# Scatter of results ahead of gather of tokens: the order of GpSimd's work in the expert loop of a mixture-of-experts layer

## The reference

```python
scores = jax.nn.sigmoid((t @ w_router).astype(jnp.float32))
_, idx = lax.top_k(scores + router_bias.astype(jnp.float32), TOP_K)
...
xb = t[row_tok].reshape(n_blocks, EXPERT_BLOCK, d)

def expert_block(args):
    xblk, e = args
    g, u = jnp.split(xblk @ w_expert_gu[e], 2, axis=-1)
    return (jax.nn.silu(g) * u) @ w_expert_down[e]

yb = lax.map(expert_block, (xb, block_e)).reshape(n_rows, d)
routed = jax.ops.segment_sum(yb * row_w[:, None].astype(yb.dtype), row_tok, num_segments=n_tok)
```

## Time and profile before

| | |
|---|---|
| median of 3 runs | 1791.23 us |
| the profiled execution's own time | 1791.92 us |
| its span | 1790.1 us |
| PE busy | 1711.8 us, 96% |
| DVE, ACT, POOL busy | 64%, 45%, 30% |
| chain that ended last | PE 71%, DMA 14% (of it the scatter 11%), DVE 5% |
| granted clock of PE | 0.991 of full |
| scatters, gathers | 102, 107 |

### The profile page before, as it was taken

One profiled execution on the slowest core, in us unless ns is written; L12 is line 12 of the kernel. 1 busy time (PEld: TensorE's weight loads), 2 busy tenths in 40 slices (PEclk: granted clock), 3 DMA queues, 4 the chain that ended last, 5 costly groups with the idle time before them and its releaser, 6 DMA issues.

```text
span 1790.1 us, 32548 instructions
## 1 busy us (share of the span) xinstructions
PE 1711.8 (96%) x7475; PEld 1239.2 (69%) x7476; DVE 1145.5 (64%) x1692; ACT 799.3 (45%) x1098; POOL 538.3 (30%) x578
## 2 busy tenths in 40 slices
PE   7999999998889999899999999999999999999997
PEld 1545454446754477688887787888888887888874
DVE  4773775403877869657538788654768578275647
ACT  0211112122231032457538787654767577265634
POOL 2000000004832320134334344334444344333442
PEclk9999999999999999999999999999999999999999
DMA  9752000011344241768959899867789789587775
GB/s 381 274 218 96 1 0 0 1 37 42 114 141 177 106 165 54 298 199 290 291 101 357 285 352 343 307 161 222 225 315 332 193 301 367 124 291 206 219 212 201
DMA packets 95503, 357.79 MB, mean 200 GB/s; under 512 B 19389, under 2 KB 19550, under 8 KB 86757
## 3 DMA queue, kind: packets, MB, share of 16 engines
q1 hardware_dynamic: 65298, 288.49, 42.3%
q0 software_dynamic: 30160, 68.76, 17.2%
q10 hardware_dynamic: 4, 0.02, 0.0%
HBM read 330.96 MB, written 70.62 MB: 224 GB/s over the span
## 4 chain that ended last, share of the span: by engine, by line
PE 71%; DMA 14%; DVE 5%; issue 4%; ACT 2%; DVEq 1%; SPq 1%; POOL 1%; ACTq 1%; POOLq 0%
DMA sum_rows<-arena,idxs 11%; PE psum L1356 7%; PE psum L1358 7%; PE psum L1357 7%; PE psum L1082 7%; PE psum L1187 5%; PE psum L1091 4%; PE psum L1343 4%; PE psum L1380 3%; PE psum L1379 3%; PE psum L1378 3%; PE psum L1029 3%; PE psum L1122 3%; DMA raw_weights<-in_w_gu 1%; ACT split_weights L698 1%
## 5 line engine op out<-in xcount | busy, mean ns | idle before, releaser
L1972 DVE TENSOR_TENSOR split_weights<-raw_weights,split_weights (+1 forms) x366 | 428.9, 1221 | 46.8 <-ACT split_weights L698 35.8
L698 ACT ACTIVATE split_weights<-raw_weights (+1 forms) x366 | 364.3, 1060 | 36.5 <-issue 24.3
L1356 PE MATMUL psum<-split_weights,split_rows 128*128 (+1 forms) x832 | 335.7, 403 | 2.3 <-DVE split_rows L1961 2.3
L1358 PE MATMUL psum<-split_weights,split_rows 128*128 (+1 forms) x832 | 325.7, 391 | 0.0
L1357 PE MATMUL psum<-split_weights,split_rows 128*128 (+1 forms) x832 | 324.9, 390 | 0.0
L698 ACT ACTIVATE arena<-psum 128x1024 f32<-128x1024 f32 (+6 forms) x187 | 154.5, 831 | 370.0 <-PE psum L1082 107.1
L654 POOL DMA_INDIRECT sum_rows<-arena,idxs x102 | 177.6, 1741 | 228.6 <-DMA sum_rows<-arena,idxs 186.4
L698 ACT ACTIVATE split_rows<-psum 128x256 fp32r<-128x256 f32 (+1 forms) x209 | 148.2, 710 | 138.4 <-PE psum L1364 124.1
L640 POOL COPY idxg<-idxT 128x1 uint32 (+1 forms) x107 | 72.8, 681 | 365.1 <-DVE split_rows L1961 292.9
L1358 PEld LDWEIGHTS psum<-split_weights,split_rows 128*128 128x128 f32 x832 | 156.8, 188 | 34.6
L1356 PEld LDWEIGHTS psum<-split_weights,split_rows 128*128 128x128 f32 x832 | 157.6, 189 | 31.5 <-DVE split_rows L1961 2.5
(11 more groups left out here) (312 smaller groups left out, 2317.8 us busy)
## 6 DMA issues: line engine op xcount, KB each, us to landing
raw_weights<-in_w_gu SPq DMA_DIRECT2D x62, 2048.0 KB
raw_weights<-in_w_dn SPq DMA_DIRECT2D x62, 1024.0 KB
arena<-in_w_ada SPq DMA_DIRECT2D x12, 2048.0 KB, 8.8
arena<-in_toks SPq DMA_DIRECT2D x18, 512.0 KB, 9.2
arena<-job_rows SPq DMA_DIRECT2D x16, 512.0 KB, 3.8
arena<-in_w_vog SPq DMA_DIRECT2D x1, 4160.0 KB, 14.2
arena<-in_w_qk SPq DMA_DIRECT2D x1, 4096.0 KB, 17.4
arena<-in_w_out SPq DMA_DIRECT2D x2, 2048.0 KB, 9.0
```

Source lines behind the costliest of these rows:

```text
L698: return act.activation(o, i, ACT.Copy)
L1356: mm(bank(3 + p), xk, part(par, 0, 512 * k), start=(k == 0), stop=False)
L1358: ins = mm(bank(3 + p), xl, part(par, 0, 512 * k), start=False, stop=(k == 7))
L1972: tt(cols(wsplit, (1 - par) * (2 * WE) + (WE + 1024 * c), 1024), cols(raw, (1 - par) * WE + 1024 * c, 1024), high, ALU.subtract).then_inc( ...
```

## The change

In the body of the loop, POOL first scatters the result of block b, and then gathers the rows of block b+5; before it was the other way round. The wait for `m_xb` moves with the gather. The counts that the two index copies wait for (6 and 7, before 7 and 6) follow from the order.

```diff
@@ -667,9 +667,9 @@
             with pool.Fori(0, rest) as i:
                 for p in range(2):
 
+                    add_rows(2 * i + p, p, 4 * i + (2 * p + 6), 16 * i + (16 + 16 * p))
                     pool.wait_ge(S("m_xb"), 2 * i + (p + 4))
-                    gather(bass.ds(2 * i + (p + 5), 1), 1 - p, 4 * i + (2 * p + 6))
-                    add_rows(2 * i + p, p, 4 * i + (2 * p + 7), 16 * i + (16 + 16 * p))
+                    gather(bass.ds(2 * i + (p + 5), 1), 1 - p, 4 * i + (2 * p + 7))
```

## The result

The changed kernel takes 1795.9 us (median of 13 runs, 1790.05 to 1802.49), the kernel before 1790.46 us (13 runs, 1787.77 to 1792.38): ratio 1.0029, 95% interval 1.002 to 1.0039. A second series gave 1.0042 (1.0028 to 1.0056). The prediction was 1787.4 us and faster; the result is slower by about 5 us and just outside the range. In this series it also varied more, 12 us between its fastest and its slowest run against 5 us before; but in a later series the kernel before itself ran from 1786.68 to 1798.54 us (15 runs), so the spread is no sign of the change.

What follows compares the result with a forecast made beforehand. PE, 96% busy, was taken to lose 14.4 us in a crowded stretch, mostly to late scatters holding ACT. Scatter waits -9.6, weights +5.8, queues and ends 0: net -3.8, 1788.1 profiled, 1787.4 us as median; range 1781.0 to 1795.5.

Steps and rivals of the forecast that it cites:

- What bounds the kernel: Crowded stretch, 955 to 1145 us: 10.15 us a step against PE's 9.35, costing 14.4 us; late scatters hold ACT.
- Scatter earlier: POOL issues the scatter at T + 2.8 instead of T + 8.6 (T: step start); waits removed are worth 9.6 us.
- Weights, 5.8 us lost again of 9.6: ACT's waits for weights replace scatter waits in the crowded stretch; 60% of the 9.6 us gain is lost again.
- net of -3.8 us: Whole kernel: 9.6 us of scatter waits removed, 5.8 us lost again to weights.
- Gather at T + 6.4 with 4.2 us of reserve: POOL's gather, now behind the scatter, lands at T + 14.5; PE wants its rows at T + 18.7.
- third rival: Gather becomes the bound and PE waits at L1343 in the crowded stretch: +6.0 us, 1797.2; chance 0.17.
- Load on the queues: Scatter goes out 0.5 us after the weights' load instead of 6: taken as 0, possible -4 to +6 us.
- The second: Rival: all returns as waits for weights, or DMA throughput sets the scatters' pace: 0 us, 1791.2; no change 0.29.
- The range and the chances: Whole kernel: 1781.0 to 1795.5 us, first rival to two thirds of third's; faster 0.45, same 0.37, slower 0.18.

Runs made afterwards that it cites:

- the profiled execution: First profile of the changed kernel, no further edit, second fastest of its 13 runs: 1790.7 us.
- the one of 1793.41 us: A further profile of the changed kernel, unaltered, from its second measurement: 1793.41 us.
- the other two: Two more profiles of the changed kernel, unaltered: 1794.04 and 1794.74 us.
- the seven versions with the full traffic: Changed kernel; it with scatter behind m_xb; split load, either order; ACT's copy about 3 or 1 us later; split load plus late copy: 1789.64 to 1811.37 us.

## Why the prediction was wrong

- **What bounds the kernel**: the place was read rightly, the crowded stretch, and without the scatter's data PE runs at full pace there. That pace is 9.42 us a step (20 groups of transposes from 962.6 to 1142.3 us in that kernel, (1142.3 - 0.8 - 962.6) / 19), not the 9.35 of the one step that I took, so the stretch had 13.2 us to give and not 14.4. The wait for the scatter came last there, but taking it away brought nothing by itself.
- **Scatter earlier**: right. T + 3.3 for T + 2.8, and no wait of ACT for it is left.
- **Weights, 5.8 us lost again of 9.6**: this step failed. In the profiled execution ACT's waits for weights rose from 11.7 to 18.7 us, near the forecast 6; but in the crowded stretch they replaced all that had gone (13.6 against 14.2 us), PE's own waits did not fall, and nothing is left of the net of -3.8 us: 980.9 against 981.0 us. With 23.9 us of these waits the loop was 2.6 us longer.
- **Gather at T + 6.4 with 4.2 us of reserve**: this step failed too, and where it shows the kernel is slower. T + 6.1 is right while the scatter before is on time, and wrong where it is not (T + 10.05 above). The prediction named that lateness and gave it no term in the sum, only a price in its third rival. In two of four executions PE waited 11.6 and 11.2 us for gathers, and the loop was 4.3 and 4.1 us longer. The way to landing was also longer than the 8.11 us taken: 9.8 us in the mean behind the nine loads that follow a pause.
- **Load on the queues, "I take 0"**: it compared a scatter 6 us behind the load with one 0.5 us behind it. That holds for undisturbed steps (6.2 us, then 0.8), and there the load got 1.6 us longer, though it met the same transfers. In the crowded stretch, where the term was to be charged, the old scatter already stood beside the load, and the loads changed by -0.5 to +0.6 us. The term was mis-sized, but no run shows that it carries the loss.
- **Rivals.** The second (all comes back as waits for weights) describes the profiled execution, and less well the one of 1793.41 us. The third (the gather as bound, 0.17, +6.0 us) describes the other two. That its price is near the measured +5.4 is chance: it added up a standstill in each step of the stretch, some 15.6 us, and there were 11.6 us in 11 steps of the whole loop. The rule of the Trainium skill on which it drew ("DMA: Bandwidth & Descriptors", "Two DMAs through the same engine are not ordered": descriptors of one queue start in order) was not tested by itself, and the gather of the earlier trace rows, which the prediction said fits it, went out before the first scatter of the loop. What the rows show is simpler: on POOL the gather's issue waits until the scatter before has landed and the next is out.
- **The range and the chances**: two thirds of the third rival's +6.0 over 1791.2 us is 1795.2, not 1795.5; the result lies outside either. 0.18 for slower was too little: two mechanisms spoke for it, and the sum had neither.

What stays open: which share of executions goes one way or the other, what decides it, and so how the 5.4 us divide between weights and gathers. Four profiles are of 1790.7 to 1794.7 us; the slower half of the runs, up to 1802.5, has no profile. Nor was it tried to send the gather through another queue, which would separate the effect on the data from the effect on the issue.

## What to carry to other kernels

Where the DMA engines are nearly full (91% here), the wait at the end of a chain need not be what costs the time: in this kernel moving a transfer ahead, or giving one more reserve, moved the wait elsewhere, and none of the seven versions with the full traffic was faster. Before moving a DMA ahead in an in-order queue, ask what it will now run beside and what is queued behind its wait. Here only less traffic helped: seven eighths of 1 MB less for each expert gave 12 us in the old order, the scatters left out 21 us.

## What the runs showed of the hardware

- A load of 2 MB that a scatter followed 0.8 us later took 9.8 to 10.0 us in the mean of nine (four profiles), one that was followed 6.2 us later 8.2 us, though both also met a gather and a load of 1 MB. In the crowded stretch, with scatters on all sides, loads took 12.1 to 13.1 us in the mean in either order.
- A shift of one copy on ACT by 1 us cost 8 us in all (1799.18 against 1790.86), while a shift by 3 us cost nothing (1789.64). Even from 766 to 955 us PE was then busy only 186.73 of 189 us (188.33 before). That short waits in the chain from ACT over DVE to PE add up is my reading of the 42 waits above and of DVE's 86 for converted weights; nothing isolates it.
- The same program on the same data goes two ways: 12.3 us of waits for weights and 11.6 for gathers in one execution, 18.7 and 1.6 in another.
